# Moving the norm, gate and hi/lo split of two branch outputs out of a stage of their own, into the stages that produce them

## What is computed

```
x += 0.5 * swiglu(rms(x))                                  # ffn1
h = rms(x);  one projection of h gives q, k, v, the gates z, ...
oa = sparse attention(...)                                 # branch A, 1152 x 512
ob = gated delta rule(...), chunk by chunk                 # branch B, 4 heads x 128
ob = ob * rsqrt(mean(ob*ob) + EPS) * norm_g * silu(z)      # norm and gate, per head and token
ya = oa @ w_branch_a ;  yb = ob @ w_branch_b
x += (sig(ga)*ya + sig(gb)*yb) @ w_out                     # merge
x += 0.5 * swiglu(rms(x)); final rms                       # ffn2
```

## Time and profile before

| | us |
|---|---|
| median of three timed executions | 3051.4 (3050.22 to 3052.1) |
| profiled execution, its own time | 3054.74 |
| its span, first to last instruction | 3052.6 |
| attend stage, about | 1502 to 1701.4 |
| delta stage | 1701.4 to 1943.08 |
| split_branches | 1943.08 to 1990.36 |
| merge | 1990.36 to 2174.5 |

### The profile page before, as it was taken

The page is one execution under the profiler, slowest core; times in us unless marked ns, Lnnn a source line. Parts: engine busy times, 40 slices in busy tenths (PEclk is TensorE's granted clock), DMA queues, the critical chain, the costliest instruction groups (busy, mean ns, idle before and its releaser), DMA issues. The chain is left out here.

```text
span 3052.6 us, 43973 instructions
## 1 busy us (share of the span) xinstructions
PE 2884.0 (94%) x16199; PEld 2709.6 (89%) x16199; DVE 1645.4 (54%) x2954; ACT 822.1 (27%) x1447; POOL 369.5 (12%) x462
## 2 busy tenths in 40 slices
PE   6999999999989999999889798699999999999998
PEld 6999999999989799999789688588889999999997
DVE  5444444444451388899254465477744444444445
ACT  4111111111132345553376321211231111111112
POOL 0000000000000045443320354300000000000000
PEclk9999999999999999999899898799999999999999
DMA  4111111111022022223200321432111111111111
GB/s 142 45 42 41 41 41 41 41 41 41 9 56 49 21 75 75 78 88 100 77 17 11 95 69 40 155 119 88 47 44 44 48 47 47 41 41 41 41 35 62
DMA packets 228844, 174.11 MB, mean 57 GB/s; under 512 B 43753, under 2 KB 208665, under 8 KB 228738
## 3 DMA queue, kind: packets, MB, share of 16 engines
q1 hardware_dynamic: 221682, 144.30, 16.4%
q10 hardware_dynamic: 4752, 18.94, 1.7%
q0 software_dynamic: 2304, 9.44, 0.9%
HBM read 137.65 MB, written 34.93 MB: 57 GB/s over the span
## 5 line engine op out<-in xcount | busy, mean ns | idle before, releaser
L506 DVE TENSOR_TENSOR ffn_prod<-ffn_silu,ffn_p_up 128x384 f32<-128x384 f32 x132 | 73.1, 554 | 769.1 <-ACT ffn_silu L426 769.1
L488 DVE SCALAR_TENSOR_TENSOR x<-ffn_p_down,x 128x512 f32<-128x512 f32 x738 | 474.8, 685 | 1.3 <-PE ffn_p_down L157 1.3
L157 PE MATMUL ffn_p_gate<-ffn_hT_hi,ffn_g_hi 128*128 128x384 f32 x1056 | 356.9, 338 | 18.0 <-ACT ffn_silu L426 10.8
L157 PE MATMUL ffn_p_gate<-ffn_hT_hi,ffn_g_lo 128*128 128x384 f32 x1056 | 355.6, 337 | 0.0
L157 PE MATMUL ffn_p_gate<-ffn_hT_lo,ffn_g_hi 128*128 128x384 f32 x1056 | 355.5, 337 | 0.0
L157 PE MATMUL ffn_p_up<-ffn_hT_hi,ffn_u_hi 128*128 128x384 f32 x1056 | 353.6, 335 | 0.0
L157 PE MATMUL ffn_p_up<-ffn_hT_hi,ffn_u_lo 128*128 128x384 f32 x1056 | 353.0, 334 | 0.0
L157 PE MATMUL ffn_p_up<-ffn_hT_lo,ffn_u_hi 128*128 128x384 f32 x1056 | 352.8, 334 | 0.0
L426 ACT ACTIVATE ffn_silu<-ffn_p_gate 128x384 f32<-128x384 f32 x132 | 64.9, 492 | 870.8 <-PE ffn_p_up L157 870.7
L157 PE MATMUL ffn_p_down<-o_c_hi,o_t_lo 128*128 128x512 f32 x756 | 295.3, 391 | 0.0
L157 PE MATMUL ffn_p_down<-o_c_lo,o_t_hi 128*128 128x512 f32 x756 | 294.8, 390 | 0.0
(11 more groups left out here) (377 smaller groups left out, 5143.7 us busy)
## 6 DMA issues: line engine op xcount, KB each, us to landing
ffn_raw_g<-in_ffn_w_gate SPq DMA_DIRECT2D x44, 512.0 KB, 5.1
ffn_raw_u<-in_ffn_w_up SPq DMA_DIRECT2D x44, 512.0 KB, 6.2
ffn_raw_d<-in_ffn_w_down SPq DMA_DIRECT2D x44, 512.0 KB, 3.6
h_raw<-in_w_in SPq DMA_DIRECT2D x32, 512.0 KB, 4.0
projected_d<-sp_stage ACTq DMA_DIRECT2D x20, 576.0 KB, 2.8
conv_d<-sp_stage ACTq DMA_DIRECT2D x12, 576.0 KB, 3.2
dl_qkv<-conv_d SPq DMA_DIRECT2D x27, 256.0 KB, 3.7
mg_gate_a<-projected_d POOLq DMA_DIRECT2D x8, 576.0 KB, 4.0
```

Of the source, the lines that this page charges most:

```text
L157: mm = nc.tensor.matmul(out, stationary(k)[a], moving(k)[b], start=(start and at == 0 and i == 0), stop=(stop and 3 * at + i == n - 1))
L488: nc.vector.scalar_tensor_tensor(out=xs, in0=p_down[(NO * q + o) % 4][:], scalar=0.5, in1=xs, op0=ALU.mult, op1=ALU.add).then_inc(added, 1)
L506: nc.vector.tensor_tensor(prod[:, slot], silu[:, slot], p_up[slot][:, 0:TG], ALU.mult).then_inc(prod_done, 1)
```

## The change

The stage split_branches is gone. What it did is spread over its neighbours:

- attend writes its output already split: ScalarE copies the rounded high part to `oT[:, 0]`, VectorE subtracts (`keep_rest`) to get the low part in `oT[:, 1]`, and both are stored, two transfers per tile in place of one. For the decoding tile: a copy, a subtraction and two stores for each half.
- delta norms, gates and splits tile by tile, two steps behind: ScalarE squares the output and copies it times the gain (`keep_outputs`); TensorE sums the squares, spread over all rows, with one matmul of 128 x 512 (`sum_squares`); ScalarE takes the root (`take_root`); POOL multiplies by the gate z, which SP loads (`gate_out`, `load_gate`); VectorE inverts the root, 128 x 512, and multiplies (`norm_out`); ScalarE rounds (`keep_high`), VectorE subtracts (`keep_rest`), SP stores both parts. `state(n)` now waits for the root, since the sums lie in its PSUM bank.
- In the SP queue of delta the store of tile n - 3 and the gate load stand behind `to_blocks(n + 2)`; before, the store of tile n - 1 stood ahead of it. `packed` comes as Y first, then X, each with a semaphore of its own, and VectorE expands Y before X and after `keep_y`.
- merge loads the four operands from DRAM by token group: `branch(0)` waits for each group's four transfers. The first weights are loaded and split at its start.

```
@@ attend, vector
+            def keep_rest(t):
+                dve.wait_ge(oT_ready, t + 1)
...
+                nc.vector.tensor_tensor(oT[:, 1], p_oT[:], oT[:, 0].bitcast(F32), ALU.subtract).then_inc(oT_rest, 1)
...
@@ delta, sync
                 if n + 1 < NT:
                     from_blocks(n + 1)
-                if 0 < n < NTP:
-                    store(n - 1)
                 if n + 2 < NT:
                     to_blocks(n + 2)
-            store(NTP - 1)
+                if n >= 3:
+                    store(n - 3)
+                    load_gate(n - 1)
...
@@ delta, tensor
             def state(n):
+                if n:
+                    pe.wait_ge(rooted, n)
...
+            def sum_squares(n):
+                pe.wait_ge(squared_out, n + 1)
+                if n < NTP - 1:
+                    pe.wait_ge(v_kept, n + 2)
+                nc.tensor.matmul(sums_of(n)[:], const.rest[:, ONES, :], square[:], start=True, stop=True).then_inc(summed, 1)
...
+                    if n >= 2 and third == 1:
+                        sum_squares(n - 2)
@@ delta, vector
+            def norm_out(n):
+                dve.wait_ge(rooted, n + 1)
+                dve.wait_ge(gated, n + 1)
+                mine = gate[:, n % 2]
+                nc.vector.reciprocal(rms[:], rms[:]).then_inc(inverted, 1)
+                dve.wait_ge(inverted, n + 1)
+                nc.vector.tensor_tensor(mine, mine, rms[:], ALU.mult).then_inc(normed, 1)
...
-                    if at == last and n + 1 < NTP:
-                        expand(n + 1, 0)
                     keep_y(n, at, 0)
                     keep_y(n, at, 1)
                     if at == last and n + 1 < NT:
                         expand(n + 1, 1)
+                    if at == last and n + 1 < NTP:
+                        expand(n + 1, 0)
...
+                    if n >= 3 and third == 0:
+                        keep_rest(n - 3)
+                if n >= 2:
+                    norm_out(n - 2)
                 if n:
                     next_state(n - 1)
...
                 add_state(h)
+                if h == 1:
+                    norm_out(NTP - 1)
+                    keep_rest(NTP - 1)
+            norm_out(NTP)
+            keep_rest(NTP)
@@ merge, sync
+            for g in range(NG):
+                if g < 2:
+                    weights.load_branches(sp, g)
+                if g == 1:
+                    weights.load_out(sp, 0)
+                mine = slice(g * TG, (g + 1) * TG)
+                for part, part_d in zip(parts, parts_d):
+                    for i in range(2):
+                        sp.dma_start(part[i][:, :, mine].bitcast(F32), part_d[i][:, :, mine].rearrange("n p t -> p n t")).then_inc(
+                            operands_in[g], 16)
@@ merge, tensor
                     pe.wait_ge(weights.ab_lo, 2 * n + 2)
+                    if n == 0:
+                        pe.wait_ge(operands_in[g], 64)
```

More of the change, by code:

```diff
@@ L1514, in _ @@
                     mask_and_top(v)
+                if u % HEADS == 3 and HEADS < u <= DEC + 3:
+                    keep_rest(u // HEADS - 1)
+                if u == DEC + 7:
+                    keep_rest_dec(0)
                 if u >= 1:
@@ L1786, in load, with load_gate @@
                         "n p t -> p n t")).then_inc(part_in[m % 2], 16)
-            def store(n):
[L1789 to L1794, removed]
+            def load_gate(n):
+                if n >= 2:
+                    sp.wait_ge(lo_done, n - 1)
+                sp.dma_start(gate[:, n % 2], projected_d[0:HB, :, n * P:(n + 1) * P].rearrange("n p t -> p n t")).then_inc(
+                    gate_in[n % 2], 16)
+            def store(n):
+                sp.wait_ge(lo_done, n + 1)
+                for i in range(2):
+                    sp.dma_start(b_parts_d[i][:, :, n * P:(n + 1) * P].rearrange("n p t -> p n t"), parts[:, i].bitcast(F32)).then_inc(
+                        parts_stored, 16)
             def to_blocks(m):
@@ L1843, in _ @@
                 sp.dma_start(new_state_s[0, :, h].rearrange("b k v -> k b v"), S_s[:, :, h, :]).then_inc(new_stored, 16)
+                if h == 1:
+                    store(NTP - 1)
+            store(NTP)
             sp.wait_ge(final_stored, 16)
             sp.wait_ge(new_stored, 16 * HB)
-            for q in range(2):
-                sp.wait_ge(out_stored[q], 16 * ((NT + 1 - q) // 2))
+            sp.wait_ge(parts_stored, 32 * NT)
         @block.tensor
@@ L2055, in _ @@
             own_outputs(0)
+            sum_squares(NTP - 2)
+            own_outputs(1)
             state(NTP - 1)
             outputs(NTP - 1)
-            for h in range(1, HB):
+            for h in range(2, HB):
                 own_outputs(h)
@@ L2248, in _ @@
             rest_of_values(NTP - 1)
+            keep_rest(NTP - 3)
             spread_values(0)
@@ L2251, in _ @@
             spread_values(1)
+            norm_out(NTP - 2)
+            keep_rest(NTP - 2)
             for h in range(HB):
@@ L2324, in step @@
                         keep_values(n - 1)
+                    if n >= 2 and third == 2:
+                        take_root(n - 2)
+                    if n >= 3 and third == 0:
+                        keep_high(n - 3)
                     if n and third == 2:
-                        keep_outputs(n - 1)
+                        keep_outputs(n - 1, p_o)
             row_exp(0)
@@ L2408, in _ @@
                     own_faded, 1)
+            gate_out(NTP)
 class MergeWeights:
@@ L2590, in merge @@
-def merge(nc, x, weights, ops, a_hi, a_lo, b_hi, b_lo, projected_d):
+def merge(nc, x, weights, ops, parts, parts_d, projected_d):
     KB = HB
@@ L2606, in merge @@
             "branches", "gated_a", "gated_b", "summed", "mhi_done", "mlo_done", "projected", "added"))
+        operands_in = [s.sem(f"operands_in{g}") for g in range(NG)]
+        (a_hi, a_lo), (b_hi, b_lo) = parts
         NO = 2 * NT
```

327 lines of the change are left out of this document (151 added, 176 removed).

## The result

The changed kernel takes 3077.8 us, median of five executions (3076.9 to 3085.2), against 3052.1 of the kernel before beside it: ratio 1.0085, 95% interval 1.0069 to 1.0101. It is slower by some 26 us. The forecast was 3058.7 with a range of 3045 to 3075: the sign is right, the size is not, and the time lies outside the range.

The account below looks back on a forecast made before the run. TensorE was taken to bound delta and merge, with split_branches' 47.3 us all on the path; terms A to G summed to +7.3 on a median of 3051.4, giving 3058.7 us, range 3045 to 3075.

Parts of the forecast that it names:

- A: Attend: the eight keep_rest hide under TensorE's work; only a last subtraction and store add, +1.4 us.
- C: Delta, steps 1 to 6: stalls for packed go, but norm_out's hold, slow clock, sum_squares and keep_rest add; net +7.4 us.
- Rival 2: Stops in delta cost more than their length, through slow matmuls and a 4.3 reciprocal: +18, or +25 with late keep_rest; 20%.
- B: Delta, first expansion: only expand Y stands between packed and z, −1.5 us.
- D: Delta, step 7: norm_out(5) ahead of next_state costs 4.1, the start 1.0 net beside own_held, sum_squares 0.9; +6 us.
- E: Tail of delta: norm_out(6) hides, norm_out(7) and norm_out(8) have no cover, 5.4 each; +12 us.
- F: Between delta and merge: the stage split_branches goes, −47.3 us.
- G: Start of merge: branch(0) waits for 13.4 MB at 350 GB/s and ends at 45.9 us, +29.3.
- rival 3: Delta's norm_out: a wide reciprocal is cheap, 0.7 to 1.7 us instead of 3.35; whole −8 to −14 us; 10%.
- the upper bound of 4.3: Delta's norm_out: the most a 128x512 reciprocal would take, in us, at 8.4 ns an element; 3.35 was taken.
- Rival 1: Merge's start: operands come at the peak rate of 413 GB/s, the whole +1.5 us, no change that can be told; 20%.
- rival 4: Delta: the change doesn't relieve the stall, packed ends as late through POOL's solve or SP waits; +12 to +18 us; 5%.

Follow-up runs that it names:

- e2: Changed kernel with attend's keep_rest of tiles 0 to 6 put one unit later in VectorE's order: 3068.2 us, ratio 1.0048.
- e3: Changed kernel with delta's keep_rest moved from behind hat_q of one round to behind keep_y of the next: 3065.7 us, ratio 1.0034.
- e9: e5 with Ln and Exp on ScalarE for root and reciprocal, w_out and later gate tiles loaded later in merge, second weights split before w_out: 3022.4 us.
- e4: Changed kernel without the reciprocal, gated output multiplied by the root (wrong results, for timing only): 3038.5 us, ratio 0.9948.
- e7: Changed kernel with 1.7 MB (w_out, gate tiles of n = 1) moved behind the last operand group at the merge's start: 3076.2 us, ratio 1.0075.
- e1: Kernel before with only lower_d's store ahead of the tile's store, and packed and its expansion Y first: 3034.9 us, ratio 0.9936.
- e5: Changed kernel with both keep_rest moves, attend's and delta's: 3062.2 us, ratio 1.0026.
- e10: e5 with norm_out, reciprocal kept, one round later behind keep_y and keep_rest at the step's end: 3037.8 us, ratio 0.9943.

## Why the prediction was wrong

**A, attend: the step that failed.** "The eight `keep_rest` on VectorE lie under TensorE's work": the subtractions do, but each began with a wait for ScalarE's copy, issued in the same unit, and behind it in VectorE's queue stood `norm`, for which TensorE waits. The term was +1.4 and measured +8.7 (8.7 to 11.4 in the kernels without e2's edit); e2 took it back.

**C, steps 1 to 6: right mechanism, one term mis-sized.** The stalls went, the hold of 4.1 came, and TensorE stopped 3.76 with 1.1 of slow clock behind it (e3's 23.87 against 19.47 in e9, less 3.34). But keep_rest stood at 0.7 a step. It was a wait of 1.2 and 0.7 to 2.0 of work ahead of keep_z, hence the second stop; with the slow matmuls behind it, it is 27.6 − 23.9 = 3.7 in the step shown, 2.9 in the mean of steps 3 to 6 (26.8). Of the 9.6 missing, steps 3 to 6 hold 8.3. Rival 2 had named this ("late keep_rest pushing keep_z of the second round too, +25"); that it was an item of a rival and not of the sum is the error, since the order of the changed kernel shows both the wait and what stands behind it. That this rival's +25 meets the measured +26 is luck: its slow matmuls of 2 a step and its reciprocal of 4.3 did not come, and the 7 of attend stood in no rival.

**B** came to −0.4 for −1.5; two profiles of one kernel differ by 3.3 there, so it can't be told. **D and E**: 17.2 for 18, in part by luck. The sum had 10 for three reciprocals and 8 for the rest. e4, without reciprocals, takes 58.1 from the z of step 7 (1889.83) to the end of delta, no more than before (58.3): all 17.4 hang on the reciprocals, with what they do to the clock, and the rest costs nothing on balance. The step's start and end, before and then after:

```profile
1886.65 3.43 PE L1990 MATMUL dl_front<-dl_kT,dl_S_s 128*128 128x16 f32 x16
1889.92 2.06 PE L1930 MATMUL dl_p_yx<-dl_Z,dl_X 128*128 128x128 f32 x8
...
1910.12 1.13 PE L1949 MATMUL dl_p_v<-dl_S,dl_kT 128*128 128x128 f32 x8 [1.49 <-DVE dl_S L2185]
```

```profile
1909.07 1.86 PE L2054 MATMUL dl_front<-dl_kT,dl_S_s 128*128 128x16 f32 x16
1914.56 2.08 PE L1985 MATMUL dl_p_yx<-dl_Z,dl_X 128*128 128x128 f32 x8 [3.63 <-DVE dl_Z L2226]
...
1940.01 2.05 PE L2004 MATMUL dl_p_v<-dl_S,dl_kT 128*128 128x128 f32 x8 [5.47 <-DVE dl_S L2275]
```

The hold at the step's end came as D has it (5.47 for 1.49). At its start `own_held` (dl_front) was to fill the stop, 1.0 net; TensorE stands 3.63 all the same. The net is 1.2 (6.38 from z to y, before 5.14) only because before, behind a stall that is gone now, `own_held` took 3.43 in place of 1.86. In E, norm_out(6) did not hide whole: TensorE stands 2.54 behind it, 1.46 in e9.

**F** as read. **G**: 46.2 for 45.9, right with its mechanism: in e7 and e9, 1.7 MB fewer ahead of the last group bring it 4.7 and 5.1 sooner. The price of the reciprocal, the unknown that I feared most, was 3.34 for 3.35; rival 3 and the upper bound of 4.3 fall. Rival 1, 413 GB/s, falls with 360, and 376 when full; rival 4 with e1 and the unstalled z of steps 3 to 7.

With A and the second stop mended (e5), the kernel takes 3062.2, and 3054 and 3057 in the two profiled executions: around the 3058.7 of the sum, whose D and E came out in part by luck.

## What to carry to other kernels

When work is spread into the idle time of a busy stage, an instruction's price on an in-order engine is its wait plus what is queued behind that wait, not its duration: ask of each moved instruction when its input is ready, and put it where the engine already waits. The same reciprocal of 3.3 us cost 4.4 us a step at one place (23.9 against 19.5 without it) and at most 1.3 one round later (20.8). Take a change apart before judging it: this one contained a gain of 18 us, and with three placements mended and a cheaper root it ends 30 us ahead of the kernel before.

## What the runs showed of the hardware

Where a TENSOR_TENSOR of VectorE with both operands in SBUF met one of 128x512 of GpSimd, one of the two was held up. Mostly it was VectorE's, which then ended 0.55 us after GpSimd's: keep_rest in the changed kernel ran from 1815.15 to 1816.83 (GpSimd until 1816.28), and in steps 4 and 5 likewise, 1.47 and 2.01 us long; in step 6, with GpSimd done 0.14 us after it began, it took 0.69. The product in e10 took 1.55 and ended 0.55 after GpSimd's too. In e10 it was also the other way round: keep_rest took 0.68, and GpSimd's product beside it 1.79:

```profile
1812.68 0.68 DVE L2264 TENSOR_TENSOR dl_parts<-dl_gate,dl_parts 128x512 fp32r<-128x512 f32 x1
1812.70 1.79 POOL L2494 TENSOR_TENSOR dl_qTe<-dl_qT,dl_e_row 128x512 f32<-128x512 f32 x1
```

The same product of GpSimd in the changed kernel took 1.27 beside a reciprocal:

```profile
1801.94 1.27 POOL L2493 TENSOR_TENSOR dl_qTe<-dl_qT,dl_e_row 128x512 f32<-128x512 f32 x1
```

Which of the two goes first is open: keep_rest began 0.02 us ahead in e10, but 0.10 ahead of GpSimd's second operation (1815.25) where it was held. The Trainium skill says of the blocking ("SBUF — State Buffer", Terms): the two engines share a pair of ports, held for a whole instruction, and the loser blocks. The trace agrees. Reciprocals (one operand) stayed at 3.34 throughout, beside GpSimd's products too.

The ten executions of e5 differ by up to 12 us, with the mean granted clock between 0.968 and 0.974; in the one pair of profiles of this kernel the 3.3 us between them lay in step 0 of delta, where the granted clock was 0.82 in one and 0.67 in the other over the same 10 us.
